# A 32-column expert arm with two gate/up units per pass, in place of the 192-column one

## What is computed

```python
logits = h @ router                       # (256, 8)
vals, idx = top_k(softmax(logits), 2)
combine = one_hot(idx) weighted by vals / sum(vals)
for e in range(8):                        # D_MODEL 1024, D_EXPERT 3584
    out += combine[..., e:e+1] * ((silu(h @ w_gate[e]) * (h @ w_up[e])) @ w_down[e])
```

## Time and profile before

| | |
|---|---|
| median of 3 runs | 1454.4 us (1453.03 to 1458.2) |
| span of the profiled execution | 1455.3 us; the page gives no other time for that execution |
| TensorE matmul busy | 1412.3 us, 97% of the span |
| VectorE, ScalarE busy | 352.0 us, 253.5 us |
| moved by DMA | 490.38 MB, mean 337 GB/s |

### The profile page before, as it was taken

The page is one execution under the profiler, slowest core; times in us unless marked ns, Lnnn a source line. Parts: engine busy times, 40 slices in busy tenths (PEclk is TensorE's granted clock), DMA queues, the critical chain, the costliest instruction groups (busy, mean ns, idle before and its releaser), DMA issues.

```text
span 1455.3 us, 23553 instructions
## 1 busy us (share of the span) xinstructions
PE 1412.3 (97%) x10068; PEld 958.1 (66%) x10068; DVE 352.0 (24%) x612; ACT 253.5 (17%) x523; POOL 48.4 (3%) x61
## 2 busy tenths in 40 slices
PE   7999999999999999989999999999999999999896
PEld 4456698884498666456479964657995563664672
DVE  3587543420147441101010000111110111110122
ACT  3245210000120032111110000221000221110221
POOL 1000001000000003000000000000000000000000
PEclk9999999999999999999999999999999999999999
DMA  9971577767669669999997577999979999999995
GB/s 381 376 301 55 227 299 269 295 234 286 231 210 379 256 226 383 426 422 426 399 423 268 224 292 300 379 425 425 425 288 384 382 426 424 425 409 407 424 425 242
DMA packets 47494, 490.38 MB, mean 337 GB/s; under 512 B 7075, under 2 KB 7795, under 8 KB 13856
## 3 DMA queue, kind: packets, MB, share of 16 engines
q1 hardware_dynamic: 39136, 468.96, 79.8%
q0 software_dynamic: 6592, 17.08, 3.2%
q10 hardware_dynamic: 1664, 2.75, 0.5%
HBM read 480.83 MB, written 13.26 MB: 340 GB/s over the span
## 4 chain that ended last, share of the span: by engine, by line
PE 88%; DMA 8%; DVE 2%; issue 1%; ACT 1%; SPq 0%; ACTq 0%; DVEq 0%
PE ps L1667 23%; PE ps L1709 15%; PE ps L1642 14%; PE ps L1405 11%; DMA ring<-stream 8%; PE ps L1368 7%; PE ps L1456 6%; PE ps L1186 4%; PE ps L1625 1%; DVE acc L805 1%; PE ps L1379 1%; PE ps L1286 1%; PE ps L1248 1%; PE ps L1302 1%; PE ps L1554 1%
## 5 line engine op out<-in xcount | busy, mean ns | idle before, releaser
L1667 PE MATMUL ps<-ring,hTe 128*64 128x256 f32 (+1 forms) x3328 | 340.3, 384 | 12.2 <-issue 8.0
L1667 PEld LDWEIGHTS ps<-ring,hTe 128*64 128x64 f32 (+1 forms) x3328 | 216.8, 132 | 115.4 <-issue 24.6
L1709 PE MATMUL ps<-ring,aT 128*32 128x256 f32 (+2 forms) x1120 | 206.7, 507 | 6.9 <-DMA ring<-stream 6.9
L1108 DVE TENSOR_TENSOR aT<-hT,ps 128x512 f32<-128x512 f32 x112 | 77.0, 688 | 547.3 <-ACT hT L680 547.3
L1642 PEld LDWEIGHTS ps<-hTe,ring 128*128 128x128 f32 x1664 | 195.1, 191 | 3.2 <-DMA ring<-stream 2.4
L1642 PE MATMUL ps<-hTe,ring 128*128 128x144 f32 (+1 forms) x1664 | 195.7, 281 | 1.5 <-DMA ring<-stream 1.5
L1709 PEld LDWEIGHTS ps<-ring,aT 128*32 128x32 f32 (+2 forms) x1120 | 77.0, 133 | 129.3 <-issue 110.3
L1405 PE MATMUL ps<-hT,ring 128*128 128x256 f32 (+1 forms) x832 | 153.5, 347 | 0.4 <-issue 0.4
L1405 PEld LDWEIGHTS ps<-hT,ring 128*128 128x128 f32 x832 | 138.0, 191 | 16.5 <-issue 1.7
L680 ACT ACTIVATE hT<-ps 128x512 f32<-128x512 f32 x112 | 66.9, 597 | 458.9 <-PE ps L1667 273.7
L805 DVE SCALAR_TENSOR_TENSOR acc<-ring,silu_c,acc 128x1024 f32<-128x1024 f32 x80 | 102.7, 1284 | 3.3 <-DMA ring<-stream 0.6
(11 more groups left out here) (228 smaller groups left out, 784.4 us busy)
## 6 DMA issues: line engine op xcount, KB each, us to landing
ring<-stream SPq DMA_DIRECT2D x182, 2048.0 KB, 14.0
acc<-stream SPq DMA_DIRECT2D x48, 1024.0 KB, 17.0
ring<-stream SPq DMA_DIRECT2D x32, 1024.0 KB, 15.7
y_store<-aT POOLq DMA_DIRECT2D x1, 8192.0 KB, 29.9
acc<-norm_w POOLq DMA_DIRECT2D x4, 512.0 KB, 12.4
y_store<-acc ACTq DMA_DIRECT2D x10, 128.0 KB, 9.6
x<-x_in SPq DMA_DIRECT2D x1, 1024.0 KB, 5.2
hTe<-ctx_in SPq DMA_DIRECT2D x1, 1024.0 KB, 23.1
```

The lines of the kernel that those rows point to most:

```text
L1108: dve.tensor_tensor(aT_e[:, u, :, :], gated_e[:, u % 2, :, :], ps[:, q:q + 2, SEQ:2 * SEQ], ALU.mult).then_inc(e_a, 1)
L1667: last = pe.matmul(to, hTe[:, k, s0:s0 + n], w, start=(k == 0), stop=(k == KD - 1))
L1709: last = pe.matmul(ps[n * r:n * (r + 1), bank, 0:cols], a_T, w[:, part * cols:(part + 1) * cols], start=(j == 0), stop=(j == NFE - 1))
```

## The change

The width 192 goes and the width 32 comes. With the counts above, experts 0 (19 tokens) and 3 (10 tokens) now take the 32-column arm; all others keep theirs. In that arm an even gate/up unit only waits until it has landed, and the odd one does both units in a single pass with four tiles, all into the PSUM bank of the odd unit; it raises `e_ps` by 2 at the end, and turns the odd unit of the pass before. A down unit is a pass of four tiles with 256 columns each.

```diff
-WIDTHS = (64, 96, 128, 144, 160, 192, 256)
-WIDE = 2
-ARMS = [("a", 64), ("a", 96), ("a", 144), ("b", 96), ("b", 64), ("a", 128), ("a", 160), ("a", 192), ("a", 256)]
+WIDTHS = (32, 64, 96, 128, 144, 160, 256)
+WIDE = 3
+ARMS = [("a", 32), ("a", 64), ("a", 96), ("a", 144), ("b", 96), ("b", 64), ("a", 128), ("a", 160), ("a", 256)]
...
-LAYOUTS = [(0, 64), (0, 128), (64, 32), (128, 32), (128, 64), (128, 128)]
+LAYOUTS = [(0, 32), (0, 64), (0, 128), (64, 32), (128, 32), (128, 128)]
...
             def done_before(width, u):
+                if width == 32 and u < GU_UNITS:
+                    return [u - 3, u - 2] if u % 2 and u >= 3 else []
                 if not is_wide(width) and any(n == 32 for _, n in BLOCKS[width]):
                     return [] if u % 2 else [u - 2, u - 1] if u else []
                 return [u - 1] if u else []
...
-                last.then_inc(eT_ps, 1)
+                last.then_inc(eT_ps, 2 if width == 32 else 1)
...
                 for u in range(GU_UNITS):
                     landed_of(e, u)
+                    if width == 32 and u % 2 == 0:
+                        landed_of(e, u, 1)
+                        continue
                     if u >= 2:
                         pe.wait_ge(e_a, e * GU_UNITS + u - 1)
+                    if width == 32 and u == 1:
+                        pe.wait_ge(hTe_dve, e * 4 + 4)
...
-                    last.then_inc(e_ps, 1)
+                    last.then_inc(e_ps, 2 if width == 32 else 1)
...
-                    if u and not is_wide(width):
+                    if width == 32:
+                        if u >= 3:
+                            turn(e, width, u - 2, 32)
+                    elif u and not is_wide(width):
                         turn(e, width, u - 1, BLOCKS[width][-1 if u % 2 else 0][1])
```

More of the change, by code:

```diff
@@ L51 @@
 TURN_AFTER = 4
-BLOCKS = {64: [(0, 64)], 96: [(0, 64), (64, 32)], 128: [(0, 128)], 144: [(0, 128), (128, 32)],
+BLOCKS = {32: [(0, 32)], 64: [(0, 64)], 96: [(0, 64), (64, 32)], 128: [(0, 128)], 144: [(0, 128), (128, 32)],
           160: [(0, 128), (128, 32)],
-          192: [(0, 128), (128, 64)], 256: [(0, 128), (128, 128)]}
+          256: [(0, 128), (128, 128)]}
 HEAD_ORDER = [h for g in range(2) for i in range(3) for h in (6 * g + i, 6 * g + 3 + i)]
@@ L444, in load_list @@
                                    by_slot[s0:s0 + n, :]).then_inc(lists_in, 16)
-            load_list(1)
+            load_list(2)
             load_list(5)
             pool.wait_ge(lists_in, 32)
-            for b, o in enumerate((1, 5)):
+            for b, o in enumerate((2, 5)):
                 last = pool.tensor_copy(token_at[:, b, :], slot_list[:, o * E:(o + 1) * E, 0])
@@ L465, in _ @@
             fetch_rows(1)
-            for o in (0, 2, 3, 4):
+            for o in (0, 1, 3, 4):
                 load_list(o)
@@ L1087, in weigh @@
                 dve.reg_alu(which, widths, 7, ALU.bitwise_and)
+                dve.reg_alu(list0, which, WIDTHS.index(64), ALU.is_ge)
                 dve.reg_alu(wide, which, WIDE, ALU.is_ge)
-                dve.reg_alu(list0, wide, E, ALU.mult)
+                dve.reg_alu(list0, list0, wide, ALU.add)
+                dve.reg_alu(list0, list0, E, ALU.mult)
                 dve.reg_alu(wide, which, WIDTHS.index(160), ALU.is_ge)
@@ L1782, in enter_first @@
                     pe.br(f"arm{width}a")
-            for width in (96, 64):
+            for width in (96, 64, 32):
                 enter_first(width)
@@ L1804, in _ @@
                               (lambda: combine(width)) if width == 64 else (lambda: pe.br(f"last{width}")))
-            for width in WIDTHS[1:]:
+            for width in [w for w in WIDTHS if w != 64]:
                 with nc.body(f"last{width}", parent=program, valid_engines=on_pe):
@@ L1808, in _ @@
                     pe.br("experts_done")
-            for width in WIDTHS[2:]:
+            for width in WIDTHS[WIDE:]:
                 enter_first(width)
```

## The result

The changed kernel takes 1462.6 us in the median of six runs (1458.8 to 1467.4), against 1454.3 for the kernel before on the same chip: the ratio is 1.0059, with an interval of 1.0041 to 1.0076. It is 8.3 us slower, a little beyond the bound of 0.5% that the prediction set, with an interval that reaches to both sides of it. The forecast was 1461.0 in a range of 1452 to 1470. The profiled execution took 1462.2 us, of which the span is 1460.3. The two spans differ by only 5.0 us (1455.3 before): a span is some 1.8 us shorter than the time of its execution, so by that estimate the profiled execution of before took about 1457.1, 2.8 above its median.

The account below looks back on a forecast made before the run. TensorE and the transfer stream were taken to bound the kernel by turns, the stream in experts 0 and 3. Terms 1.6 + 1.9 + 1.0 + 2.0 + 1.0 - 0.6 = +6.9 us on 1454.4 gave 1461, range 1452 to 1470.

Parts of the forecast that it names:

- The work removed: Experts 0 and 3: 39 us of TensorE time saved in each, all under the stream, worth 0.
- The new wait: 32-column arm: one bank makes each pass wait 3.2 us for turn, silus, copy and product; a pair takes 6.7 us.
- Restart in expert 3: Expert 3: places come back late and the queue runs empty twice, 1.6 us and 1.9 us.
- The first hole: Expert 3, pass 3: starts at 934.3 after a slowed pass 2, leaving 1.6 us of empty queue.
- The second term: Expert 3, pass 7: hands back unit 16's place late after partly slowed passes, 1.9 us more of empty queue.
- Restart in expert 0: Expert 0, after pass 1: issues come at 546.2, the queue is empty for 2 us, already lost 1.0: +1.0 us.
- The next expert's start: Expert 4 should begin at a slowed clock, +2.0 us; expert 1 already began slowed, no change.
- The jumps: Behind the arms of experts 0 and 3: the next arm no longer lies next in memory, +1.0 us for two.
- stores: Experts 0 and 3: stores shrink from 256 to 128 KB in each, -0.6 us.
- Nothing changes: Rival: the clock holds through 3.2 us gaps and the jumps are covered; 1454 to 1457 us, chance 0.18.
- Slowed all along: Rival: every gap lowers the clock, pairs take over 10 us; +12 to +21 us, 1466 to 1475, chance 0.14.
- Faster: Rival: places return in pairs and the queue never runs dry, pass 2 before 544; 1450 to 1453 us, chance 0.06.

Follow-up runs that it names:

- two_banks: Changed kernel with the 32-column arm's passes alternating between two PSUM banks, and one silu, copy and product per pass: 1458.6 us, ratio 1.0033.
- only_e3: Changed kernel with the 32-column arm's threshold at 15 tokens, so only expert 3 takes it and expert 0 the 64-column arm: 1464.2 us, ratio 1.0070.
- warm: Changed kernel with 30 transposes that nobody reads after each 32-column arm, ahead of the branch: 1472.8 us, ratio 1.0119.
- chain_warm: The run chain with 50 transposes that nobody reads behind each 32-column arm: 1453.2 us, ratio 0.9989.
- chain: The run all_pad with a second 64-column arm behind expert 6's 96-column arm, so expert 7's code lies next in memory: 1456.6 us, ratio 1.0012.
- adjacent: Changed kernel with the arms that follow experts 0 and 3 laid next in memory, using two copies of the 32-column arm: 1463.4 us, ratio 1.0062.
- all_pad: Changed kernel with two_banks, adjacent and the address shift of adj_pad together: 1455.6 us, ratio 1.0013.
- adj_pad: The run adjacent with each 32-column arm meant to sit 128 instructions further into its 256-instruction block: 1463.8 us, ratio 1.0064.
- all_pad_warm: The run all_pad with 30 transposes that nobody reads behind each 32-column arm: 1455.9 us, ratio 1.0008.

## Why the prediction was right, and where it was not

**The work removed was worth nothing.** Right, and only its size was off: in the two experts 58.8 us of TensorE time went, where 78 were forecast (the 62.7 of the page include 3.9 from other stages). A gate/up pass takes 3.66 and not 3.5 us, a down pass 1.93 at the full clock and 3.3 to 3.6 when slowed, where 1.75 was forecast. Expert 0 is as long as before, expert 3 longer.

**The new wait.** Right. The pair was forecast at 6.7 us and takes 6.78, by the chain named for it.

**Restart in expert 3.** The first hole is right in place, cause and size: pass 2 ran at the lowered clock (0.68 over 923 to 927), pass 3 began at 931.85 and its place was issued at 933.18, for 1.6 us of empty queue. Two of its terms were off and nearly cancelled: TensorE stood still for 2.89 us before pass 2 and not 4.5, but the first pass took 5.25 us and not 3.5, with 0.97 us of stall in it that I had not counted. The second term failed in its cause. The prediction said "the next two places come at pass 3"; in fact pass 3 hands back the places of units 2 and 3, and of these only that of unit 3 goes to the next unit in the queue (10), while unit 2's is kept for unit 15. One unit feeds the queue for 4.93 us, and units 11 and 12 are issued only at pass 4, 7.67 us after unit 10: hence the hole at 940 to 944, 2.4 us, that I had not seen. Of the 7.67 us 1.4 are the slowed clock of pass 3. The forecast hole at unit 16, 1.9 us, did not come (the share of DMA is 1.01 from 964 to 999), since the later passes kept the full clock. So the whole, +3.5 forecast and +4.0 measured, came near by luck: a hole that did not come stands against one that I had not seen. That the holes are the work of the single bank's handshake, slowed clock included, is shown by two_banks, which brings the landing back to 79.8.

**Restart in expert 0.** Forecast +1.0. Expert 0 is 83.2 us long in both profiles although it now ends with 1.20 us of late start, so the landing of expert 1's unit came no later but 1.2 sooner; in only_e3, where expert 0 has the old arm, the stretch is 82.5. Versions with the same arm there lie between 80.6 and 83.3 (warm apart), so one profile can't tell 1 us; the term was no larger than that. The queue does run low here (131 GB/s over 546 to 549), but over the first 50 us of the expert it moved 379 GB/s in both kernels. All seven passes of expert 0 took 3.66 us, so no slowed clock delayed them.

**The next expert's start.** Forecast +2.0, measured +2.2 (152.3 against 150.1), right in cause too: the stretch at 1002 has the clock at 0.50, and in chain_warm, with no gap ahead of it, the clock is 1.00 and the 150.1 come back. I had read the rule on oscillation that I cited from the Trainium skill, page "TensorE: Matmul & The Clock Gate", as saying that every pass would be slow. It speaks of compute shorter than the wait for data, and the gate/up passes, 3.66 us behind gaps of 2.9, are longer than theirs: two of the seven in expert 3 were slow, none in expert 0. The down passes, 1.93 us of work behind waits of up to 2.96, are nearer to its case, and even there two of the four from 969.47 took 3.26 and 3.48 us and two 1.93. The measurement decides: not every tile met the slow clock.

**The jumps.** Too small. Forecast +1.0 for two; they showed 1.20 ahead of expert 1 and 2.55 ahead of expert 4. I had the last down pass end 3.2 us ahead of the landing and the jump covered all but 0.3 to 0.5 of its 3.5. The step that failed is the price of the jump: the last down matmul ended 3.93 us ahead of the landing of expert 4's unit, more than forecast, and the first matmul came 6.49 us behind it, where I had taken 3.53. In warm it came 5.2 us behind the end of the transposes. Adjacency removes all of it at expert 1 and about half at expert 4. The Trainium skill, page "Runtime: NRT & Kernel Launch", section "Instruction fetch mechanics", says that code is fetched ahead in sequence and that a taken branch out of what is loaded fetches its target first. This agrees with expert 1 (1.20 down to 0.0) and with chain (3.5 down to 0), but alone it doesn't give the 1.2 to 1.8 us that are left ahead of expert 4 when its code lies next. The traces show what ends that rest: in adjacent and all_pad too a 16 KB transfer of instructions begins only after the last down matmul, 2.95 and 2.6 us behind it, and the first matmul follows 2.8 us later (the table in the last section). Why the transfer begins so late stays open.

**The sum.** In experts 3 and 4, holes less stores 4.3, the late start 2.5 and the slow start 2.2 make the +9.0 of the profiles, where 3.2, 0.5 and 2.0 were forecast. The 3.3 us that were missing are 2.0 of the jump, 1.1 of the holes and 0.2 of the clock. Expert 0 gave back 1.2 (its restart, its jump and its stores, forecast at +1.2, together show 0.0), which leaves 2.1, and 9.0 is the +6.9 of the forecast with it. That the forecast of 1461.0 lies within 2 us of 1462.6 owes something to luck, since a jump priced too low stands against a loss in expert 0 that was not seen.

**The rivals.** None came. "Nothing changes" fell with the first hole. "Slowed all along" was wrong in that only passes 2 and 3 of expert 3 were slowed; in adj_pad and warm, where three were, expert 3 takes 88.9 and 94.2, so it was nearer than its chance said. "Faster" needed pass 2 of expert 0 before 544, with the expert's start at 539.39, which is 4.6 us behind it. It began at 543.33, but in an execution whose expert 0 starts at 537.64: 5.7 us behind the start, the second half of unit 8 was issued later than before, and the queue did run low.

## What to carry to other kernels

Ask of each stage what ends it before making it shorter: an arm that the stream ends gains nothing from faster matmuls by themselves, and can lose through later returns of buffers, a colder clock and less cover for the branch behind it. When two units share a pass, write down for each pass which buffers it hands back and for which transfer each of them is kept, since the queue stops at the first that is missing, not at their number. A stall at an engine is worth removing only if the chain that ends the stage runs through it (expert 7's 3.5 us did not), and work that was put in to hold the clock did so here only where it ran up to the first matmul (chain_warm), not with 2.32 us of pause behind it (all_pad_warm). Look also at where such work moves the code that lies behind it (warm).

## What the runs showed of the hardware

- The same gap did not always have the same effect on TensorE's clock. In expert 3 a gap of 2.90 us stands before a pass of 5.03 us and before one of 3.66. In expert 0 of the same run no pass behind such a gap was slowed; in adj_pad two were there, and three in expert 3. I had slowed half of the passes by such gaps; what decides between them is open.
- The time from a branch to the first matmul of the next arm is not one figure. It showed as nothing behind the landing at expert 1 when the code lay next, as 1.2 to 1.8 us behind the landing at expert 4 when it lay next and 2.1 to 2.6 when it did not, as some 3.5 us at expert 7 in full view, and in warm as 5.2 us between the last transpose and the first matmul. Around the start of expert 4 the trace has 16 KB transfers of instructions in the middle of the saturated stream, at 998.90 and 1005.08; before the change they began at 989.76 and 995.87.
- A late start follows the transfer of its code. In all ten versions that run the 32-column arm, a 16 KB instruction transfer begins 2.71 to 2.85 us ahead of expert 4's first matmul, wherever the landing and the end of the arm lie. Seven of them:

| us | last down matmul ends | transfer begins | first matmul |
|---|---|---|---|
| after | 995.19 | 998.90 | 1001.67 |
| adjacent | 995.58 | 998.53 | 1001.38 |
| adj_pad | 1001.57 | 1004.52 | 1007.29 |
| two_banks | 994.02 | 997.41 | 1000.20 |
| all_pad | 989.33 | 991.94 | 994.72 |
| warm (transposes to 1007.51) | 1004.08 | 1009.99 | 1012.70 |
| chain_warm (transposes to 997.68) | 992.08 | 994.91 | 997.64 |

  Expert 7 shows the same: 2.73 us in the kernel before, 2.73 in the changed one, each with some 3.5 us of idle time; in chain, where its code lies next and nothing is idle, the last transfer began 9.76 us ahead of the start. Before the change expert 4 had one 7.0 us ahead and one 0.9, and started at its landing. No run moved the transfer alone, so that the start waits for it is read from this regularity. Where expert 4's code lay next, the transfer began 2.6 to 3.0 us behind the last down matmul, else 3.4 to 3.7 (warm apart).
- 50 transposes of 128x128 took 5.68 us, 30 took 3.49. In chain_warm, with no gap behind the 50, the clock was 1.00 in expert 4; in all_pad_warm, with 2.32 us between the last of the 30 and the start, expert 4 was no shorter than without them.
